# Mixture-of-experts stage: the two last experts' results kept on chip, the first expert's rows picked by matrix products, one place table

## The reference, cut to what matters

```python
h = rms_norm_2(x, norm_ffn_g) * (1.0 + sc_f) + sh_f
p_g = softmax(h @ w_rg + b_rg); g_sel = argmax(p_g)            # one of 4 groups
e_logits = (h @ w_re + b_re) of that group                      # 8 experts
top_p, top_i = top_k(softmax(e_logits), 2)                      # two experts a token
weights = top_p / sum(top_p) * p_g[g_sel]
y[token] = sum over its 2 experts of
           weight * ((silu(h @ w_gate[e]) * (h @ w_up[e])) @ w_down[e])
x = x + g_f * y
return rms_norm_2(x, final_norm_g)
```

## Time and profile before

| | |
|---|---|
| median of 3 runs | 1473.2 us (1470.58 to 1477.06) |
| the profiled execution, its own time | 1470.04 us |
| its span in the trace | 1468.0 us |
| TensorE busy | 1328.4 us, 90% of the span |
| VectorE / ScalarE / GpSimd busy | 572.7 / 345.2 / 158.7 us |
| memory read / written | 296.08 MB / 13.73 MB |
| mean granted TensorE clock | 0.951 of full |

### The profile page before, as it was taken

How to read it: one execution, slowest core, us unless ns; L and a number is a source line. 1 busy time by engine, 2 the same in 40 slices (tenths; PEclk the granted TensorE clock), 3 DMA queues, 4 the chain that set the end, 5 groups by cost and what they waited for, 6 DMA issues and landing times.

```text
span 1468.0 us, 21300 instructions
## 1 busy us (share of the span) xinstructions
PE 1328.4 (90%) x7646; PEld 658.7 (45%) x7647; DVE 572.7 (39%) x1078; ACT 345.2 (24%) x745; POOL 158.7 (11%) x273
## 2 busy tenths in 40 slices
PE   5989999999999989998999896699899878998887
PEld 2445656568844444446455444333333322333222
DVE  1366373735123343468566734322212121122124
ACT  2222232321234432211454421011101010111012
POOL 4011111102020000000000001211111111111110
PEclk9999999999999999998999997699989999999999
DMA  9151607051171100121110384169999999999994
GB/s 353 72 202 42 256 2 287 2 201 32 30 243 56 33 15 0 34 86 44 58 58 1 129 372 193 36 273 393 401 420 417 408 402 419 423 393 409 411 389 198
DMA packets 40768, 300.71 MB, mean 205 GB/s; under 512 B 8840, under 2 KB 8992, under 8 KB 23792
## 3 DMA queue, kind: packets, MB, share of 16 engines
q1 hardware_dynamic: 32704, 285.12, 49.4%
q0 software_dynamic: 7984, 14.50, 3.3%
HBM read 296.08 MB, written 13.73 MB: 211 GB/s over the span
## 4 chain that ended last, share of the span: by engine, by line
PE 72%; DMA 17%; DVE 7%; issue 2%; ACT 1%; POOL 0%; SPq 0%; DVEq 0%; ACTq 0%; POOLq 0%
PE bank L832 21%; DMA arena<-in_w_down 12%; PE bank L2744 10%; PE bank L763 8%; PE bank L2760 7%; PE bank L878 4%; DVE arena L2167 3%; DMA arena<-in_w_gu 3%; PE bank L841 2%; PE bank L821 2%; DMA arena<-in_w_ada 2%; PE bank L2734 1%; DMA arena<-in_ada_w 1%; PE bank L1060 1%; PE bank L1076 1%
## 5 line engine op out<-in xcount | busy, mean ns | idle before, releaser
L832 PE MATMUL bank<-hT,arena 128*128 128x512 f32 x768 | 341.7, 600 | 0.0
L2744 PE MATMUL bank<-arena,hT 128*64 128x512 f32 x1024 | 233.9, 606 | 24.2 <-DMA arena<-in_w_gu 22.7
L832 PEld LDWEIGHTS bank<-hT,arena 128*128 128x128 f32 x768 | 144.6, 192 | 177.3 <-issue 174.9
L2744 PEld LDWEIGHTS bank<-arena,hT 128*64 128x64 f32 x1024 | 72.0, 139 | 164.4 <-issue 139.1
L2760 PE MATMUL bank<-arena,yT 128*64 128x512 f32 x512 | 128.7, 649 | 14.5 <-DMA arena<-in_w_down 14.4
L763 PE MATMUL bank<-arena,yT 128*128 128x512 f32 x256 | 114.4, 602 | 2.3 <-DVE yT L1633 2.3
L2904 DVE TENSOR_SCALAR hT<-hT 128x256 f32<-128x256 f32 x32 | 9.4, 294 | 247.1 <-ACT hT L2855 247.1
L763 PEld LDWEIGHTS bank<-arena,yT 128*128 128x128 f32 x256 | 48.2, 193 | 60.5 <-issue 56.2
L2760 PEld LDWEIGHTS bank<-arena,yT 128*64 128x64 f32 x512 | 36.7, 148 | 82.3 <-issue 64.6
L878 PEld LDWEIGHTS bank<-arena 64*64 64x64 f32 x1856 | 59.3, 135 | 27.9 <-issue 14.4
L2855 ACT ACTIVATE hT<-bank 128x256 f32<-128x256 f32 x32 | 12.3, 383 | 246.2 <-PE bank L2744 246.2
(11 more groups left out here) (471 smaller groups left out, 1592.1 us busy)
## 6 DMA issues: line engine op xcount, KB each, us to landing
arena<-in_w_gu SPq DMA_DIRECT2D x64, 2048.0 KB, 30.7
arena<-in_w_down SPq DMA_DIRECT2D x32, 2048.0 KB, 36.6
arena<-in_w_in SPq DMA_DIRECT2D x55, 512.0 KB, 3.7
arena<-in_ada_w SPq DMA_DIRECT2D x24, 1024.0 KB, 5.0
arena<-in_w_ada SPq DMA_DIRECT2D x8, 1024.0 KB, 9.1
arena<-in_w_out SPq DMA_DIRECT2D x8, 1024.0 KB, 14.3
arena<-in_w_ada SPq DMA_DIRECT2D x8, 512.0 KB, 4.7
arena<-expert_rows SPq DMA_DIRECT2D x4, 1024.0 KB, 8.4
```

What stands on the lines that cost most here:

```text
L832: last = T.matmul(bank[0:rows, :], w[:, k, 0:rows], hT[:, k, :], start=k == 0, stop=k == KD - 1)
L2744: last = T.matmul(banks[1 + ub][MT * h:MT * h + MT, :], tile.xT[:, k, :], wgu[u][:, k // 4, :, k % 4, 256 * h:256 * h + 256], start=k == 0 ...
```

## The change

1. **Expert 0 without a gather.** All four tiles of normalised rows now stay on chip (columns 8192 to 12287 of `arena`, the down part of slot 2). TensorE picks expert 0's rows itself: for each of 8 column groups, 4 products of the 128 x 128 rows with `first_hot` (128 x 64), 32 products, straight in turned form, so that the transposes go too. `first_hot` costs VectorE two instructions (`hot_of`) ahead of those for `slots`. TensorE raises the semaphores that let the gathers begin ahead of these products.
2. **Loads.** Since the rows lie in slot 2, down(2) is sent once the products are done; down(1) moves behind the storing of `xn_dram`, since the gate of the second block's output lies in slot 1 now (that gate's own load waits for the last z projection).
3. **One place table.** Places are choice x 512 + token, so the token table serves for the places too: 8 more products instead of 16, behind the 32 products, and `dve_places` after `rows_in` of expert 0. Two more VectorE instructions stand ahead of the first `s_routed`. `y_dram` is read back as two 4 KB pieces a token instead of one of 8 KB.
4. **Two last experts on chip.** Expert 30 is not scattered either; a second scatter of zero rows is sent at the start. `last_hot` exists twice; the turning (16 products, up from 8) moves from the start into the last turn, with the spreading of the gain. The reading back waits for the scatter of expert 29.
5. **The last turn.** Loads go gate/up(31), down(30), down(31). TensorE does spread, gate/up(31), down(30), turning of 31's hidden values, `add_x(3)`, three `add_last`, down(31), then the sums, with five more `add_last`.

```diff
@@ dve_router
+            eng.sem_inc(s_hot, 1)
+            hot_of(0, first_hot)
             eng.sem_inc(s_hot, 1)
...
+        def hot_of(e, out):
+            dve.done(V.scalar_tensor_tensor(hot_last, hot_pos, 0.0, hot_tile[:, :, e:e + 1].to_broadcast([P, KT, MT]), ALU.is_gt, MUL))
+            dve.done(V.tensor_tensor(out, hot_last[:, 0:TT, :], hot_last[:, TT:KT, :], ADD))
@@ sp_experts
-            for u in range(U):
-                eng.wait_ge(s_slots, 2 if u < 2 else 3)
-                load_gate_up(u, u)
-                load_down(u, u)
+            eng.wait_ge(s_slots, 2)
+            load_gate_up(0, 0)
+            load_down(0, 0)
+            load_gate_up(1, 1)
+            eng.wait_ge(s_slots, 3)
+            load_down(1, 1)
+            load_gate_up(2, 2)
+            eng.wait_ge(tiles[0].xf, 2)
+            load_down(2, 2)
...
-            eng.wait_ge(extra.stored, 16)
-            for u in (1, 2, 0):
-                eng.wait_ge(tiles[u].stored, 16 * (ROUNDS + (u < REST - 1)))
+            eng.wait_ge(extra.stored, 32)
+            for u in range(U):
+                eng.wait_ge(tiles[u].stored, 16 * ROUNDS)
@@ pool_experts
-            done(G.tensor_copy(place_col[:, U + 1:U + 2], places[:, NE - 1:NE]))
-            eng.indirect_dma_start(y_half, ...place_col[:, U + 1:U + 2]..., extra.yo, ...).then_inc(extra.stored, 16)
+            done(G.tensor_copy(place_col[:, U + 1:U + 3], places[:, NE - 2:NE]))
+            for j in range(2):
+                eng.indirect_dma_start(y_half, ...place_col[:, U + 1 + j:U + 2 + j]..., extra.yo, ...).then_inc(extra.stored, 16)
@@ pe_experts
+            eng.wait_ge(s_hot, 2)
+            for k in range(KD):
+                for t in range(TT):
+                    last = T.matmul(banks[ROWS_BANK][:, MT * k:MT * k + MT], xn_tiles[1][t][:, k::KD], first_hot[:, t, :],
+                                    start=t == 0, stop=t == TT - 1)
+            last.then_inc(tiles[0].xf, 1)
+            for by in ("act", "dve"):
+                eng.wait_ge(emptied[by], len(given[by]))
+            for n in range(KT):
+                last = T.matmul(banks[4][MT:P, 0:NE + NOV], hot_pos[:, n, :], hot_tile[:, n, :], start=n == 0, stop=n == KT - 1)
+            last.then_inc(s_spread, 1)
...
                 if last:
-                    finish(it0, u0, e - 1)
-                    spread_gain()
+                    spread()
                 gate_up(tiles[u], first, u, e, u, it)
...
-                if not begun and not last:
+                if last:
+                    eng.wait_ge(s_copied, 1)
+                    overflow(it, u, e)
+                if not begun:
                     finish(it0, u0, e - 1)
...
             experts(eng, body)
             turn_hidden(tiles[LAST[1]], first, NE - 1)
             add_x(3, False)
+            eng.wait_ge(first.rows, NE - 1)
+            add_last(0, 0, start=True)
+            add_last(0, 3)
+            eng.wait_ge(first.hidT, NE)
+            add_last(0, 1, start=True)
             finish(LAST[0], LAST[1], NE - 1)
             sums()
```

More of the change, by code:

```diff
@@ L2126, in pe_block2 @@
             full(last)
[L2127 to L2132, removed]
         s_y2, s_chosen, s_hot = sem("y2_made"), sem("experts_chosen"), sem("slots_hot")
@@ L2483, in dve_router @@
+            done(V.tensor_tensor(v, v, v2, ADD))
             done(V.tensor_copy(slots[:, 0:NE + NOV], v))
             eng.sem_inc(s_routed, 1)
[L2485 to L2490, removed]
@@ L2581, in extras @@
                     body(o)
+        ROWS_BANK = 7 if bank_of[fill_at[("slots",)]] == 0 else 0
         def sp_experts(eng):
@@ L2683, in body @@
                     eng.wait_ge(tiles[u2].xf, it2 + 1)
[L2684 to L2688, removed]
+                    gather(tiles[u2], u2, e + 2, s_picked[0], e + 1)
+                extras(eng, e, more)
+                if not (isinstance(e, int) and e in (0, NE - 1)):
                     it0, u0 = before(it, u)
                     scatter(tiles[u0], first, u0, e - 1, s_placed_col[0], e - 1)
[L2691 to L2695, removed]
+            eng.wait_ge(tiles[1].xf, 1)
+            gather(tiles[1], 1, 1, s_picked[0], 0)
             done(G.memset(extra.xg, 0.0))
@@ L2797, in body, with spread @@
                     turn_rows(tiles[u1], first, e + 1, it1)
-                if not begun and not last:
+                if last:
+                    eng.wait_ge(s_copied, 1)
+                    overflow(it, u, e)
+                if not begun:
                     finish(it0, u0, e - 1)
[L2800 to L2804, removed]
+                if not last:
+                    overflow(it, u, e)
+            def spread():
                 eng.wait_ge(s_gateB, 16 + 48)
                 for half in range(2):
-                    spread = T.matmul(banks[4 * half][:, :], ones_row, gain_row[:, 512 * half:512 * half + 512], start=True, stop=True)
-                spread.then_inc(s_spread, 1)
+                    T.matmul(banks[half][:, :], ones_row, gain_row[:, 512 * half:512 * half + 512], start=True, stop=True)
+                eng.wait_ge(s_routed, 3)
+                for j in range(2):
+                    for t in range(TT):
+                        for q in range(2):
+                            ins = T.matmul(banks[3 + 2 * j][MT * q:MT * q + MT, CH(t)], last_hot[j][:, t, :], ident[:, :], start=True, stop=True)
+                ins.then_inc(s_spread, 1)
             def add_x(t, stop):
@@ L2839, in sums @@
                 ins.then_inc(s_x3, 1)
-            eng.wait_ge(s_routed, 3)
-            for t in range(TT):
-                for q in range(2):
-                    turned = T.matmul(banks[6][MT * q:MT * q + MT, CH(t)], last_hot[:, t, :], ident[:, :], start=True, stop=True)
-            turned.then_inc(s_spread, 1)
-            turn_rows(tiles[0], first, 0, 0)
             experts(eng, body)
@@ L2871, in body @@
                     eng.wait_ge(s_spread, 2)
[L2872 to L2873 removed]
+                    for j in range(2):
+                        S.activation(finalG[:, 512 * j:512 * j + 512], banks[j][:, :], ACT.Copy)
+                        last = S.activation(last_sel[:, j, :, :].rearrange("p t n -> p (t n)"), banks[3 + 2 * j][:, :], ACT.Copy)
                     last.then_inc(s_copied, 1)
@@ L2927, in body @@
                     rows_in(extra, more_, 0, 0, 5)
-                    eng.wait_ge(extra.stored, 16)
+                    eng.wait_ge(extra.stored, 32)
                 if last:
-                    rows_gated(tiles[u0], first, u0, e - 1, it0)
                     for k in range(2):
@@ L2947, in body @@
                 extras(eng, e, more)
-            rows_in(tiles[0], first, 0, 0)
+                if last:
+                    rows_gated(tiles[u0], first, u0, e - 1, it0)
+            rows_in(tiles[0], first, 0, 0, ROWS_BANK)
+            dve_places(eng)
             eng.wait_ge(s_gateB, 16 + 48)
```

134 lines of the change are left out of this document (63 added, 71 removed).

## The result

The changed kernel takes 1475.15 us (median of 12 runs, 1471.26 to 1482.56), the kernel before, run beside it 12 times, 1469.97 us. The ratio is 1.0036 with an interval of 1.0019 to 1.0054: slower, by 3 to 8 us, and by the median inside the 0.5% that was called no change (the interval ends just outside). Forecast was 1475.5, as +2.3 us on a median of 1473.2; against the longer series of before it is +5.2. So the time was met, the difference was not quite, and it is the difference that has to be explained.

The account below looks back on a forecast made before the run. Weight loading was taken to bound the experts, leaving the start and the TensorE work at the end: +2.5 - 0.2 = +2.3 us on a median of 1473.2, 1475.5 us. Range 1466.5 to 1481; the forecast's own 1473 to 1479.5.

Parts of the forecast that it names:

- DMA-bound middle: From the first reload on, expert weights load at 404 GB/s with full queues; the change leaves this stretch as it is.
- The 32 products, 14.6 us at half clock: At the start, expert 0's row-picking products: 64 records at half clock, priced from L2095; 7.5 us at full clock.
- Rival A: At the start the products warm TensorE to full clock; with the end -5.4 us, 1467.8 us; chance 0.22.
- Gate/up of expert 0 at +3.1 us: At the start, gate/up of expert 0 begins at 939.7 us, 3.1 us later than before.
- The gains by the clock afterwards: After the products, gate/up of expert 0 takes 0.6 us less by an earlier clock rise; the extra tile's 8.78 stays.
- the reload: First reload of slot 0, which moves all the rest: from 958.24 to about 960.7 us, the start's +2.5 us.
- The moved waits: At the start, moved VectorE steps, zero scatters and later down loads stay hidden; the loads' price is nothing.
- The end, -0.2 us: From the last loads to the last sum, TensorE work is only dealt out otherwise: 1461.0 us, before 1461.2.
- C: Rival at the end: keeping expert 30 on chip wins nothing, which the sum already includes; chance 0.06.
- B: Rival at the end: the reading back takes the weights' bandwidth and delays down(31), at most 6.9 us, 1482.6 us; chance 0.07.
- The base: Median of the kernel before, 1473.2 us, to which the forecast difference of +2.3 us was added.
- +4.3: Upper bound of the start's +2.5 us: products at 15.7 us and nothing won by the clock.

Follow-up runs that it names:

- e9: Changed kernel with more products of no use, 8 instead of e7's 4 ahead of the slots products; the 32 products took 15.49 us.
- e3: Changed kernel with only expert 31 on chip and the end's loads, last turn and sums as before; ratio 1.0007 to the kernel before.
- e12: Kernel before, unedited, run once for a third profile; 1471.63 us.
- e8: Changed kernel with expert 0 gathered and the last sums in the old order, both last experts on chip; ratio 0.9971 to the kernel before.
- e10: Changed kernel with rows picked as in e6 and the last sums in the old order; median 1467.85 us.
- e11: Changed kernel with nothing but the last sums in the old order; by the medians it gives some 2 to 3 us.
- e1: Changed kernel unedited, run again beside the kernel before; ratio 1.0049.
- e5: e2 with only expert 31 on chip and the end as before the change; 0.5 us faster than e2 by the medians.
- e2: Changed kernel with expert 0's rows gathered again, the gather let off early; ratio 0.9967 to the kernel before.
- e6: Changed kernel with the one-hot matrix as weights and rows moving, 512 columns at a time; gate/up begins 11.1 us after the slots products.
- e7: Changed kernel with products of no use, 3 ahead of the rank products and 4 ahead of the slots products; the clock fell after 4.1 idle us.

## Why the prediction was right, and where it wasn't

- **DMA-bound middle:** right. From the first reload to the last load that TensorE waits for it is 477.2 and 478.7 us in the changed kernel, 476.7 to 479.0 in the three profiles before. So the middle did not move with the change, but it varies by some 2 us from one execution to the next.
- **The 32 products, 14.6 us at half clock (14.4 to 15.7):** the size was right (15.5), and at half clock the likeness to L2095 held, load for load (335 and 333 ns). What was wrong is the belief that the full clock would halve their time. Rival A (-5.4 us, chance 0.22) rested on 117 ns a record at full clock, and e9 shows 235, so A's price was wrong, and the low side of the range too wide for that reason. That the clock stays at 0.50 through them was right. The rule behind A (the Trainium skill, TensorE: Matmul & The Clock Gate, Part 1, sustained matmul activity brings the full clock) isn't borne out by these 15.5 us.
- **Gate/up of expert 0 at +3.1 us:** measured +3.5 (18.9 against 15.4); the products took 0.9 more than summed, the rest 0.5 less. The gains by the clock afterwards were under-sized: -1.7 and -1.7 in the profiled pair, for -0.6 and 0. The one for gate/up stands in every profile (8.4 and 8.4 us changed, 9.6 to 10.1 before), the one for the extra tile is chance (7.1 in four of the five, 8.8 in the first one before). Against all three profiles before, the reload comes 0.1 to 2.5 us later, predicted +2.5.
- **The moved waits:** right. The zero scatters held nothing; down(2) at 944.19 and down(1) cost nothing.
- **The end, -0.2 us:** the failing term. Down(30) to the end of down(31) came out as worked out (12.1 us). Behind it I had 14.0 and it is 15.3: a lone `add_last` 1.06 instead of 0.9 (0.6 in all five), `add_x` 1.91 instead of 1.77 (0.4), the diagonals 3.7 instead of 3.5; the bare wait was 0.8 as priced. And the old end, 26.3 in the earlier trace rows, had a clock penalty of 1.6 in it, which e3 and e12 show absent. The -0.2 was reckoned against that one execution. So the term is +1.1 to +2.7. e8, e10 and e11 take 1.8 of it back by order alone.
- **C, keeping expert 30 on chip wins nothing:** right; with its order of sums it costs, 4.0 us of the medians in e3 against e1, but only 0.5 in e5 against e2.
- **B:** didn't occur; the reading back was sent at 1439.74 and down(31) found its weights.
- **The base.** 1473.2 was a median of three; twelve give 1469.97. My +2.3 landed on the time since the base was 3.2 too high and the difference some 3 too low, which is luck. (Of the bounds, +4.3 adds up to +4.2, and 1479.5 to 1479.3; nothing hangs on it.)

The profiles put the change at +3.4 us (549.3 against 545.8, the means of two and of three, from the `slots` products on). The medians say +5.2 and +4.9. Some 1.5 us are not settled: the early part falls out as chance, and what is left is less than the middle alone varies by.

## What to carry to other kernels

Before replacing a transfer by products, look at what lets the transfer off: here a gather let off 4 us sooner, with the work in its way shortened and moved, brought gate/up 4.5 us forward, and the products that should do away with the gather cost 15. Price matmuls from rows with the same weight access, not only the same size, before you count on a faster clock. Try the other operand as the weights: in e6 that brought gate/up 7.8 us forward, though it changed the number of records, the columns and the access all at once. In a chain of sums at the end, keep products of one shape together and put one that needs nothing in front of the wait: here 1.8 us in the profiles.

## What the runs showed of the hardware

- fp32 products with 128x128 weights. Columns side by side: loads of 192 ns at 1.00 and 333 at 0.50 (L2091 of the changed kernel), 117 and 225 ns a record. Columns 32 bytes apart: loads of 335 ns at either clock, 235 ns a record at 1.00 (11 records, e9) and 242 at 0.50. The same strided columns in transposes load in 188 ns, 226 at most.
- 15.5 us of such products without a gap didn't raise the clock in any of five profiled executions (of the changed kernel, e1, e3, e7 and e11), and it fell during them in e9, where it stood at 1.00. It rose 2.8 us into the 5.1 us of products with 512 moving columns (e6), and 1.9 us into them in e10.
- The same part of one program ran at full clock in one execution and partly at half in another (1.00 against means of 0.75 and 0.60), worth up to 7 us of 1470. One profiled pair can't carry a difference of this size; spans from a common mark can.
